# Three feed-forward blocks of a fused kernel: output parts of 6, 8 and 8 chunks, VectorE's order by need, and two of four weight sums made by accumulating transfers

## The chip, the cores and the metric

The kernel runs on one core of one Trainium2 chip. The time is the device time of one execution in microseconds (us), the median of the runs shown. Engines are named as in the profile: PE (TensorE; PEld is its weight load), DVE (VectorE), ACT (ScalarE), POOL (GpSimd) and SP (SyncE, which here only issues transfers).

## The reference, cut to what matters

Two transformer blocks follow each other on a sequence of 512 tokens of width 1024, all in float32. The first has a gated linear attention mixer and a feed-forward block (ffn0); the second a feed-forward block (ffn1), a mixer of pooling and retention, and a feed-forward block (ffn2), then a last norm.

```python
def swiglu_2(x, w1, w3, w2):                       # w1, w3: 1024 x 2816, w2: 2816 x 1024
    return (jax.nn.silu(x @ w1) * (x @ w3)) @ w2

# first block, after its mixer
h = modulate(rms_norm(lat, norm_g[i, 2]), mod_l[:, 3], mod_l[:, 4])
lat = lat + mod_l[:, 5] * rms_norm(swiglu(h, ffn_w_in[i], ffn_w_out[i]), norm_g[i, 3])
# second block
h = h + 0.5 * swiglu_2(rmsnorm(h, ffn1_norm[l]), ffn1_w1[l], ffn1_w3[l], ffn1_w2[l])
...  # mixer
h = h + 0.5 * swiglu_2(rmsnorm(h, ffn2_norm[l]), ffn2_w1[l], ffn2_w3[l], ffn2_w2[l])
return rmsnorm(h, final_norm)
```

## The kernel before, in words

**Numbers in two parts.** Each float32 operand is split into an upper part (ACT copies it to the type fp32r) and a lower part (DVE subtracts the upper from the whole). A product is three matmuls: upper by upper, upper by lower, lower by upper (`mm3`). So every weight tile passes ACT once and DVE once before PE takes it; `hi_done`/`lo_done` count this for whole units, `form_hi`/`form_lo` for forms.

**One ffn** has 11 groups of 256 hidden columns. Groups 0 and 1 (`PLAIN`) are plain: `unit(0, ...)` makes the gate half and `unit(1, ...)` the up half, in ffn0 and ffn1 group 0 runs as `first_pair`, which takes the chunks k of x as they come (`PAIR_ORDER`). Groups 2 to 10 are `pair`s: gate and up weights, each cut into two halves of the inputs (h) and two of the outputs (c), are multiplied with x by Winograd's form of Strassen's scheme, with 7 products of half size instead of 8. Product j takes the weight form j and the x form j (`x_form`). Weight forms 0, 1 and 5 are blocks of the loaded weights as they are. Four are sums, made in place by DVE in `form_sum`: form 3 = block (0,1) + block (1,1), kept in `sum_form[0]`; form 4 = block (0,0) + block (0,1); form 2 = form 4 + block (1,1); form 6 = form 2 + block (1,0), in `sum_form[1]`. `raw_pair[h]` holds the loaded half h of both weights (1 MB each). The 7 x forms need four sums of x quarters (`sum_x`), an upper part by ACT (`x_hi`) and a lower part by DVE (`x_lo`).

**Stretches and output parts.** The pairs run in stretches of 3, 4 and 2; after each stretch an output part multiplies 8, 8 and 6 of the 22 hidden chunks (128 rows of w_out each) with w_out, in four steps jj of 256 output columns, `OUT_PAIRS`. In the third part the last two chunks (group 10) come late: PE does jj 0 and 1 without them, waits for `gated`, and does them after.

**Buffers that tie the engines.** A ring of four slots holds the weight forms. ACT may write form j of a pair when PE has finished the product four forms before (`form_used`). SP loads `raw_pair[0]` of the next pair when DVE has lowered form 4 of this one (`form_lo`), and `raw_pair[1]` when it has lowered form 5. PE takes product 2 of a pair when DVE has lowered form 2 (`form_lo`).

**Order around the change.** Each engine's instructions are written out by hand and run in that order; a wait holds up all that stands behind it on its engine. The changed places are the opening of each ffn on DVE and ACT (from `scale_x` to the first `pair`), `pair` and `first_forms` on DVE, the third output part on PE, the end of ffn0 on DVE, and how the inverse roots of the norm are spread over the partitions before ffn1, the mixer and ffn2 (`broadcast` of a diagonal made by DVE, or `spread_roots` straight from the roots that POOL made). `keep_busy(b, n)` issues n idle matmuls.

## Time and profile before

| | |
|---|---|
| median of 3 runs | 1604.76 us (1600.16, 1604.76, 1604.80) |
| the profiled execution's own time | 1599.87 us |
| its span, first to last instruction | 1598.1 us |
| PE, DVE, ACT, POOL busy | 98%, 70%, 42%, 8% |
| granted TensorE clock, mean | 0.991 |
| moved by DMA | 172 MB, 108 GB/s |

A row of a timeline begins with its start and its duration in us; the bracket at its end is idle time of that engine before the row and what ended it. A row of the waits has the total, the number of waits and the longest. Most of the time lies in matmuls that follow each other without a gap; what can be won without taking matmuls away is in the gaps of PE and in the stretches at half clock.

### The profile page before, as it was taken

How to read it: one execution, taken by the hardware profiler on the slowest of the kernel's cores; microseconds unless marked ns; L12 is line 12 of the kernel's file. 1: busy time of each engine (PE TensorE's matmuls, PEld its weight loads, DVE VectorE, ACT ScalarE, POOL GpSimd, SP SyncE). 2: the span in 40 equal slices, each digit the busy share in tenths (PEclk: the TensorE clock that was granted, in tenths of full speed). 3: DMA queues.
4: the chain of work that ended last, by engine and by line, in shares of the span. 5: the costliest groups of instructions: out<-in, count | busy, mean ns of one | idle time of the engine just before them, and what ended most of it. 6: DMA issues, size and time to landing. Idle time of an engine off the chain costs nothing.

```text
span 1598.1 us, 23120 instructions
## 1 busy us (share of the span) xinstructions
PE 1566.3 (98%) x9784; PEld 1411.7 (88%) x9784; DVE 1113.7 (70%) x1284; ACT 670.6 (42%) x848; POOL 122.4 (8%) x106
## 2 busy tenths in 40 slices
PE   9999999999999999989999999999999999999997
PEld 7888888889989989778989989888988799899896
DVE  5898764688748746788847856666457786587466
ACT  4554375554525514525524533421323354254242
POOL 0100000020000000000000000175006000000000
PEclk9999999999999999999999999999999999999999
DMA  9544511221412322303231332343212222223131
GB/s 387 198 157 158 211 53 53 80 79 54 158 53 106 131 81 93 119 27 99 84 135 55 105 132 80 106 146 105 80 53 80 79 106 106 82 92 145 53 117 69
DMA packets 35879, 172.05 MB, mean 108 GB/s; under 512 B 3008, under 2 KB 5312, under 8 KB 26176
## 3 DMA queue, kind: packets, MB, share of 16 engines
q1 hardware_dynamic: 31424, 153.80, 26.9%
q0 software_dynamic: 4352, 16.78, 3.1%
q8 instruction: 77, 1.26, 0.3%
q14 instruction: 26, 0.21, 0.0%
HBM read 168.47 MB, written 2.10 MB: 107 GB/s over the span
## 4 chain that ended last, share of the span: by engine, by line
PE 86%; DVE 8%; DMA 2%; issue 2%; ACT 1%; POOL 0%; DVEq 0%; POOLq 0%; ACTq 0%
PE bank L585 86%; DMA raw_pair<-in_ffn_in 2%; DVE form_slot L2504 2%; DVE sum_form L2498 1%; DVE hs L2462 1%; DVE raw_pair L2498 1%; ACT form_slot L1709 0%; DVE x_form L2478 0%; DVE unit_slot L2539 0%; DVE both L2451 0%; DVE w_all L1898 0%; DVE kd L2297 0%; DVE both L2277 0%; DVE both L2429 0%; PE bank L940 0%
## 5 line engine op out<-in xcount | busy, mean ns | idle before, releaser
L585 PE MATMUL bank<-x_form,form_slot 128*128 128x256 f32 x4536 | 548.6, 284 | 6.8 <-DVE form_slot L2504 5.4
L585 PEld LDWEIGHTS bank<-x_form,form_slot 128*128 128x128 f32 x4536 | 547.4, 193 | 8.6 <-issue 5.8
L585 PE MATMUL bank<-g_slot,unit_slot 128*128 128x512 f32 (+1 forms) x1614 | 362.2, 385 | 4.8 <-DVE unit_slot L2539 3.0
L585 PEld LDWEIGHTS bank<-g_slot,unit_slot 128*128 128x128 f32 x1614 | 298.3, 188 | 66.0 <-DVE unit_slot L2539 3.9
L1709 ACT ACTIVATE form_slot<-raw_pair 128x1024 fp32r<-128x1024 f32 x135 | 140.8, 1054 | 244.8 <-PE bank L585 147.5
L585 PE MATMUL bank<-a_hi,w_all 128*128 128x512 f32 x768 | 235.9, 396 | 6.6 <-DVE w_all L1898 6.4
L2504 DVE TENSOR_TENSOR form_slot<-raw_pair,form_slot 128x1024 fp32r<-128x1024 f32 x135 | 164.1, 1221 | 64.4 <-ACT form_slot L1709 64.3
L585 PEld LDWEIGHTS bank<-a_hi,w_all 128*128 128x128 f32 x768 | 144.3, 189 | 39.2 <-issue 9.3
L585 PE MATMUL bank<-a_lo,w_all 128*128 128x512 f32 x384 | 142.6, 392 | 0.0
L1898 DVE TENSOR_TENSOR w_all<-w_raw,w_all 128x2048 fp32r<-128x2048 f32 x38 | 90.1, 2371 | 47.4 <-ACT w_all L1378 47.3
L2539 DVE TENSOR_TENSOR unit_slot<-w_raw,unit_slot 128x2048 fp32r<-128x2048 f32 (+1 forms) x36 | 77.0, 2139 | 60.3 <-ACT unit_slot L1728 44.7
L1728 ACT ACTIVATE unit_slot<-w_raw 128x2048 fp32r<-128x2048 f32 (+1 forms) x36 | 63.7, 1770 | 127.6 <-PE bank L585 127.6
L1378 ACT ACTIVATE w_all<-w_raw 128x2048 fp32r<-128x2048 f32 x40 | 76.5, 1912 | 93.5 <-PE bank L585 93.5
L585 PE MATMUL bank<-w_all,a_hi 128*128 128x512 f32 (+1 forms) x384 | 108.8, 359 | 0.0
L490 POOL TENSOR_TENSOR root<-col,power 128x4 f32<-128x4 f32 (+2 forms) x15 | 18.3, 1222 | 977.2 <-DVE col L1925 776.7
L585 PEld LDWEIGHTS bank<-a_lo,w_all 128*128 128x128 f32 x384 | 72.7, 189 | 15.5 <-issue 0.5
L585 PE MATMUL bank<-w_all,a_lo 128*128 128x256 f32 (+1 forms) x256 | 78.7, 308 | 0.0
L585 PEld LDWEIGHTS bank<-w_all,a_hi 128*128 128x128 f32 x384 | 67.7, 189 | 10.2
L2498 DVE TENSOR_TENSOR sum_form<-raw_pair,raw_pair 128x1024 f32<-128x1024 f32 x54 | 66.0, 1222 | 9.9 <-DMA raw_pair<-in_ffn_in 8.7
L2588 DVE SCALAR_TENSOR_TENSOR xT<-bank,xT 128x512 f32<-128x512 f32 x32 | 22.1, 689 | 72.7 <-PE bank L585 72.7
L2504 DVE TENSOR_TENSOR form_slot<-sum_form,form_slot 128x1024 fp32r<-128x1024 f32 x54 | 65.7, 1216 | 9.9 <-ACT form_slot L1709 9.8
L1709 ACT ACTIVATE form_slot<-sum_form 128x1024 fp32r<-128x1024 f32 x54 | 56.5, 1047 | 0.0
(314 smaller groups left out, 1850.1 us busy)
## 6 DMA issues: line engine op xcount, KB each, us to landing
raw_pair<-in_ffn_in SPq DMA_DIRECT2D x54, 1024.0 KB, 5.2
w_raw<-in_ffn_out SPq DMA_DIRECT2D x24, 1024.0 KB, 4.9
mod_raw<-in_mod POOLq DMA_DIRECT2D x16, 1024.0 KB, 5.6
w_raw<-in_ffn_in SPq DMA_DIRECT2D x12, 1024.0 KB, 4.9
w_raw<-in_gla_in SPq DMA_DIRECT2D x10, 1024.0 KB, 5.7
w_raw<-in_mix_in SPq DMA_DIRECT2D x10, 1024.0 KB, 4.9
w_raw<-in_ffn_out SPq DMA_DIRECT2D x12, 768.0 KB, 4.2
mod_w<-in_mod SPq DMA_DIRECT2D x8, 1024.0 KB, 18.2
```

The source lines that it names most:

```text
L490: nc.gpsimd.tensor_tensor(root4[:, c0:c0 + n], col4[:, c0:c0 + n], power[:, 0:n], ALU.pow).then_inc(root_done, 1)
L585: return pe.matmul(out, lhs, rhs, start=first, stop=last, skip_group_check=True)
L1378: nc.scalar.activation(flat(w_hi[s]), flat(w_raw[s]), ACT.Copy).then_inc(hi_done[s], 1)
L1709: nc.scalar.activation(ring[(STRETCH_SLOT[q] + at) % 4][:, 0], form_source(j), ACT.Copy).then_inc(form_hi, 1)
L1728: nc.scalar.activation(flat(unit_slot[(PART_SLOT[q] + 2 * jj) % 4])[:, 0:w], flat(w_raw[s])[:, 0:w], ACT.Copy).then_inc(hi_done[s], 1)
L1898: V.tensor_tensor(flat(w_lo[s]), flat(w_raw[s]), flat(w_hi[s]).bitcast(F32), ALU.subtract).then_inc(lo_done[s], 1)
L2462: V.scalar_tensor_tensor(hs[:, m], xT[:, m], gains(m), roots[:], ALU.mult, ALU.mult).then_inc(hs_done, 1)
L2498: V.tensor_tensor(out, x, y, ALU.add).then_inc(form_summed, 1)
L2504: V.tensor_tensor(slot[:, 1], form_source(j), slot[:, 0].bitcast(F32), ALU.subtract).then_inc(form_lo, 1)
L2539: V.tensor_tensor(flat(unit_slot[(at + 1) % 4])[:, 0:w], flat(w_raw[s])[:, 0:w], flat(unit_slot[at % 4])[:, 0:w].bitcast(F32), ALU.subtrac ...
L2588: done = V.scalar_tensor_tensor(xT[:, m], b[:], 0.5, xT[:, m], ALU.mult, ALU.add)
```

## The change

- Stretches of 2, 4 and 3 pairs, output parts of 6, 8 and 8 chunks; the slots of the ring, of the output weights and of the gated values are moved to fit. In the third part only jj 0 is cut in two around the wait for group 10; jj 1 to 3 run whole.
- Forms 3 and 4 are no longer summed by DVE. SP loads block (0,1) once more, alone, into `sum_form[0]` (two transfers of 256 KB, in pieces of 512 bytes), as soon as form 3 of the pair before is lowered. POOL waits for it and adds block (1,1) from HBM with two accumulating transfers; then it waits for `raw_pair[0]` and adds block (0,0) from HBM onto block (0,1) in it, with two more. ACT's form 3 waits for `sum_moved[0]`, its form 4 and DVE's sum for form 2 for `sum_moved[1]`.
- On DVE the opening of each ffn is put in another order; the x forms 2 to 6 are lowered one by one inside the first pair.
- The roots come by `spread_roots`: in ffn1 after chunk (0,3) instead of (0,5), before ffn2 and the mixer after the fourth product of the second unit instead of the eighth, without the diagonal. The 20 idle matmuls before ffn1 become 8.
- At the end of ffn0 the last output chunk (m = 7) is added after the terms of chunk 6.

VectorE, opening of ffn1: `hs` is `scale_x`, `x_sum` is `sum_x`, `w_all` the lower part of a unit's weights (w_raw_49 for `lo_done[0]`, w_raw_50 for `lo_done[1]`), `x_form` is `x_lo`, `both<-bank,roots` scales a gate or an up half. Before:

```order
L2462 SCALAR_TENSOR_TENSOR hs<-xT,cols,roots 128x512 x8
L2467 TENSOR_TENSOR x_sum<-hs 128x4x256
L2469 SCALAR_TENSOR_TENSOR x_sum<-x_sum,hs 128x4x256
L2471 TENSOR_TENSOR x_sum<-hs,x_sum 128x4x256
L2472 TENSOR_TENSOR x_sum<-hs 128x4x256
L2429 TENSOR_TENSOR both<-bank,roots 128x512 x2
L1898 TENSOR_TENSOR w_all<-w_raw_49,w_all 128x2048
L2440 TENSOR_TENSOR both<-bank,roots 128x512 x2
L2451 TENSOR_TENSOR both<-both 128x1024
L1898 TENSOR_TENSOR w_all<-w_raw_50,w_all 128x2048
```

and now:

```order
L2485 SCALAR_TENSOR_TENSOR hs<-xT,cols,roots 128x512 x8
L2452 TENSOR_TENSOR both<-bank,roots 128x512 x2
L1922 TENSOR_TENSOR w_all<-w_raw_49,w_all 128x2048
L2463 TENSOR_TENSOR both<-bank,roots 128x512 x2
L2490 TENSOR_TENSOR x_sum<-hs 128x4x256
L2492 SCALAR_TENSOR_TENSOR x_sum<-x_sum,hs 128x4x256
L2494 TENSOR_TENSOR x_sum<-hs,x_sum 128x4x256
L2495 TENSOR_TENSOR x_sum<-hs 128x4x256
L2474 TENSOR_TENSOR both<-both 128x1024
L1922 TENSOR_TENSOR w_all<-w_raw_50,w_all 128x2048
```

The weights of the unit that PE takes next now stand ahead of the four sums.

VectorE, from form 6 of one pair to form 4 of the next: `raw_pair_60`, `raw_pair_61` are halves 0 and 1, `sum_form_70` is form 3, `sum_form_71` form 6. Before:

```order
L2504 TENSOR_TENSOR form_slot_63<-sum_form_71,form_slot_63 128x1024
L2504 TENSOR_TENSOR form_slot_64<-raw_pair_60,form_slot_64 128x1024
L2498 TENSOR_TENSOR sum_form_70<-raw_pair_60,raw_pair_61 128x1024
L2498 TENSOR_TENSOR raw_pair_60<-raw_pair_60 128x8x128
L2504 TENSOR_TENSOR form_slot_65<-raw_pair_61,form_slot_65 128x1024
L2523 SCALAR_TENSOR_TENSOR both<-kd_159,ke_160 128x2x256
L2526 TENSOR_TENSOR both<-bank,kd_159 128x2x256
L2498 TENSOR_TENSOR raw_pair_60<-raw_pair_60,raw_pair_61 128x8x128
L2498 TENSOR_TENSOR sum_form_71<-raw_pair_60,raw_pair_61 128x1024
L2504 TENSOR_TENSOR form_slot_62<-raw_pair_60,form_slot_62 128x1024
L2529 TENSOR_TENSOR both<-bank,snap_b 128x2x256
```

and now:

```order
L2520 TENSOR_TENSOR form_slot_62<-sum_form_71,form_slot_62 128x1024
L2520 TENSOR_TENSOR form_slot_63<-raw_pair_60,form_slot_63 128x1024
L2520 TENSOR_TENSOR form_slot_64<-raw_pair_61,form_slot_64 128x1024
L2537 SCALAR_TENSOR_TENSOR both<-kd_160,ke_161 128x2x256
L2540 TENSOR_TENSOR both<-bank,kd_160 128x2x256
L2514 TENSOR_TENSOR raw_pair_60<-raw_pair_60,raw_pair_61 128x8x128
L2514 TENSOR_TENSOR sum_form_71<-raw_pair_60,raw_pair_61 128x1024
```

Two of the four sums are gone from VectorE; the sum for form 2 stays where it was. GpSimd has in their place, once for each of the 27 pairs:

```order
L525 DMA sum_form_70<-in_ffn_in 128x4x128 x2
L528 DMA raw_pair_60<-in_ffn_in 128x4x128 x2
```

The diff, cut:

```diff
-STRETCHES = ((2, 3, 4), (5, 6, 7, 8), (9, 10))
+STRETCHES = ((2, 3), (4, 5, 6, 7), (8, 9, 10))
-OUT_PARTS = ((0, 8), (8, 16), (16, 22))
-PART_SLOT = (1, 1, 0)
-PART_NEEDS = (4, 8, 11)
+OUT_PARTS = ((0, 6), (6, 14), (14, 22))
+PART_SLOT = (2, 2, 0)
+PART_NEEDS = (3, 7, 11)
...
@@ sync, ffn
                         n = PAIRS_PER_FFN * f + i - PLAIN
+                        if n:
+                            sp.wait_ge(form_lo, FORMS * n - 3)
+                        for u in range(2):
+                            sp.dma_start(form_source(3)[:, u], weight_block(w_in, i, 0, 1)[:, u]).then_inc(sum_begun, 16)
                         for h in range(2):
@@ gpsimd
+            def form_sums(f, w_in):
+                for q, groups in enumerate(STRETCHES):
+                    for i in groups:
+                        n = PAIRS_PER_FFN * f + i - PLAIN
+                        pool.wait_ge(sum_begun, begun_before + 32 * (n + 1))
+                        for u in range(2):
+                            pool.dma_start(form_source(3)[:, u], weight_block(w_in, i, 1, 1)[:, u], accum_op=ALU.add).then_inc(sum_moved[0], 16)
+                        pool.wait_ge(raw_loaded[0], 16 * (RAW_BEFORE[f] + i + 1 + 2 * q))
+                        for u in range(2):
+                            pool.dma_start(form_source(4)[:, u], weight_block(w_in, i, 0, 0)[:, u], accum_op=ALU.add).then_inc(sum_moved[1], 16)
@@ tensor, unit
-                    if roots_to is not None and order.index((k, c)) == KD - 1:
-                        broadcast(roots_to, T, tmp[3], roots_spread)
+                    if roots_to is not None and order.index((k, c)) == KD // 2 - 1:
+                        spread_roots(roots_to, 0, roots_spread)
@@ tensor, group
-                        first_pair(*((3 * KD, (0, 5)) if scaled else (2 * KD,)))
+                        first_pair(*((3 * KD, (0, 3)) if scaled else (2 * KD,)))
@@ tensor, third output part
-                    for jj in range(2):
-                        pe.wait_ge(lo_done[jj], cnt.next(lo_done[jj]))
-                        out_banks_free(q, jj)
-                        out_products(q, jj, k0, late)
-                    pe.wait_ge(gated, GROUPS * f + PART_NEEDS[q])
-                    for jj in range(2):
-                        out_products(q, jj, late, k1)
-                        cnt.expect(pair_out[jj])
-                    for jj in (2, 3):
+                    for jj in range(OUT_PAIRS):
                         s = jj % 2
                         pe.wait_ge(lo_done[s], cnt.next(lo_done[s]))
                         out_banks_free(q, jj)
-                        if f == 2 and jj == 3:
-                            out_products(q, jj, k0, k0 + 1)
-                            last_part(s, k0 + 1)
+                        if jj == 0:
+                            out_products(q, jj, k0, late)
+                            pe.wait_ge(gated, GROUPS * f + PART_NEEDS[q])
+                            out_products(q, jj, late, k1)
+                        elif f == 2 and jj == 3:
+                            out_products(q, jj, k0, KF - 5)
+                            last_part(s, KF - 5)
...
-            keep_busy(0, 20)
+            keep_busy(0, 8)
@@ scalar, form_upper
+                    elif j in (3, 4):
+                        act.wait_ge(sum_moved[j - 3], moved_before + 32 * (n + 1))
@@ vector, form_sum (the sums for forms 3 and 4 are gone)
+                        dve.wait_ge(sum_moved[1], moved_before + 32 * (n + 1))
                         dve.wait_ge(form_lo, FORMS * n + 1)
                         out, x, y = form_source(2), form_source(4), form_source(5)
```

## Rows read from the trace of the kernel before

**Rows 1.** The page, part 1: busy time, share and instructions.

```profile
PE 1566.3 (98%) x9784; PEld 1411.7 (88%) x9784; DVE 1113.7 (70%) x1284; ACT 670.6 (42%) x848; POOL 122.4 (8%) x106
```

**Rows 2.** Waits of PE over the span: total us, times, longest.

```profile
PE bank L585 <- DVE w_all L1898: 6.4, 1, 6.4
PE bank L585 <- DVE form_slot L2504: 5.4, 1, 5.4
PE bank L585 <- DVE unit_slot L2539: 3.0, 2, 1.9
PE bank L585 <- DVE qd L2297: 3.0, 1, 3.0
PE bank L585 <- ACT both L1614: 1.8, 1, 1.8
```

**Rows 3.** Timeline of PE from the end of ffn0 into ffn1.

```profile
672.65 2.21 PE L585 MATMUL bank<-g_slot,unit_slot 128*128 128x512 f32 x9
...
680.57 1.05 PE L585 MATMUL bank<-ones,qd 128*128 128x1 f32 x8 [3.03 <-DVE qd L2297]
...
687.09 5.48 PE L585 MATMUL bank<-ones 128*128 128x128 f32 x40
...
706.07 1.05 PE L585 MATMUL bank<-ident,root 128*128 128x128 f32 x8
...
721.70 0.77 PE L585 MATMUL bank<-a_hi,w_all 128*128 128x512 f32 x1 [6.39 <-DVE w_all L1898]
```

**Rows 4.** Timeline of DVE in the same stretch.

```profile
687.40 0.69 DVE L2336 TENSOR_TENSOR y_ffn<-y_ffn,bank 128x512 f32<-128x512 f32 x1 [2.50 <-PE bank L585]
...
702.85 1.63 DVE L2387 SCALAR_TENSOR_TENSOR a_lo<-xT,cols,a_hi 128x512 fp32r<-128x512 f32 x2
707.86 5.39 DVE L2462 SCALAR_TENSOR_TENSOR hs<-xT,cols,roots 128x512 f32<-128x512 f32 x8 [3.38 <-ACT roots L1640]
713.28 1.23 DVE L2467 TENSOR_TENSOR x_sum<-hs 128x1024 f32<-128x1024 f32 x1
...
719.27 2.28 DVE L1898 TENSOR_TENSOR w_all<-w_raw,w_all 128x2048 fp32r<-128x2048 f32 x1
```

**Rows 5.** Stretches: length, busy PE, PEld, DVE, ACT, POOL; granted clock, DMA share, GB/s.

```profile
870.42:890.58 20.16, 20.16 (x171) 20.16 (x169) 16.12 (x15) 11.48 (x13) 0.00 (x0) 1.00 0.31 105
721.70:726.40 4.70, 4.70 (x11) 3.77 (x12) 4.60 (x5) 4.30 (x5) 0.00 (x0) 0.50 0.70 212
1282.08:1286.20 4.12, 4.12 (x19) 4.12 (x20) 4.09 (x5) 1.96 (x2) 0.00 (x0) 0.50 0.00 0
```

**Rows 6.** Timeline of PE in the third output parts of ffn0, ffn1 and ffn2.

```profile
658.26 2.08 PE L585 MATMUL bank<-g_slot,unit_slot 128*128 128x512 f32 x8 [1.79 <-ACT both L1614]
...
1034.28 2.11 PE L585 MATMUL bank<-g_slot,unit_slot 128*128 128x512 f32 x8 [1.10 <-DVE unit_slot L2539]
...
1570.93 1.42 PE L585 MATMUL bank<-g_slot,unit_slot 128*128 128x512 f32 x5 [1.95 <-DVE unit_slot L2539]
```

**Rows 7.** Timeline of DVE at the opening of ffn2.

```profile
1271.52 4.56 DVE L2478 TENSOR_TENSOR x_form<-x_sum,x_form 128x1024 fp32r<-128x1024 f32 x4
```

**Rows 8.** Timelines of DVE and PE in the stretch of four pairs of ffn1.

```profile
876.40 1.23 DVE L2504 TENSOR_TENSOR form_slot<-raw_pair,form_slot 128x1024 fp32r<-128x1024 f32 x1 [0.94 <-ACT form_slot L1709]
...
891.94 1.21 DVE L2498 TENSOR_TENSOR raw_pair<-raw_pair,raw_pair 128x1024 f32<-128x1024 f32 x1
...
917.58 6.01 PE L585 MATMUL bank<-x_form,form_slot 128*128 128x256 f32 x48 [0.72 <-ACT snap_a L1716]
```

**Rows 9.** Tile raw_pair, 856 to 924 us: from SP's issue to landing.

```profile
DMA to landing us min/median/max: 5.5/6.1/7.2
```

**Rows 10.** Tile mod_raw (POOL's own loads, 1 MB each), and POOL's queue on the page.

```profile
L519 POOL DMA_DIRECT2D mod_raw<-in_mod x16: 748/748/952, 49.3 to 175.5; - x16
DMA to landing us min/median/max: 5.4/5.6/7.4
q0 software_dynamic: 4352, 16.78, 3.1%
```

90 lines of the change are left out of this document (51 added, 39 removed).

## The prediction

> **What bounds the kernel now.** I read the page first: PE is busy 98% of a span of 1598.1 us, DVE 70% [rows 1]. The change takes away no matmul of the products, so a gain can only come from PE's idle time, from its half clock and from idle matmuls. Then I read PE's waits: five causes make 19.6 us [rows 2], and the timelines say where each lies. Two are at the openings of ffn1 and ffn2 (6.4 and 5.4 us, for DVE), one at the end of ffn0 (3.0 us, for the last sum over y), three in the third output parts (1.79, 1.10 and 1.95 us) [rows 6]. After the two openings the granted clock is 0.50 for 4.70 and 4.12 us of work [rows 5], after PE had stood still for 6.39 and 5.44 us. Inside a stretch of pairs a pair takes 20.16 us, PE is busy all of it and DVE 16.12 us of it [rows 5].
>
> The profiled execution took 1599.87 us, 1.8 more than its span; the median of the runs is 4.9 higher. I make the sum on the span and set it against the median. A difference of about 0.3% (5 us) is what a measurement of this kernel can tell from no change.
>
> **Third output parts.** Before, PE does jj 0 and 1 without the last two chunks, then both late pieces at once, so that both finish almost together and the weights and banks of jj 2 and 3 are asked for before ACT and DVE have them. Now only jj 0 is cut. One chunk of one jj is 6 matmuls; 9 of this kind take 2.21 us [rows 3], so a chunk takes 1.36 us and a jj of 8 chunks 10.9 us, where one of 6 took 8.2. Behind the last pair, DVE and ACT need for group 10 a combine, silu, product, its upper and its lower part: 0.7 + 1.1 + 1.2 + 1.1 + 1.2, and 0.8 because ACT copies the weights of jj 1 in between: 6.1 us, an estimate, under the 8.2 us of six chunks. The lower weights of jj 1 follow at 8.4, needed at 10.9. Each later jj gives DVE 10.9 us for work that it did in 8.2. All three waits go: 4.8 us; at worst, if group 10 is late by more than 2 us, half of it comes back.
>
> **End of ffn0.** PE's last product ends at 672.65 + 2.21 = 674.86; DVE starts to scale y by the roots at 687.40 [rows 3, 4]: 12.5 us. In between DVE adds chunks 6 and 7, then eight term operations, and only then has PE what it sums. Now chunk 6 and its terms are done while PE still multiplies chunk 7. DVE's queue behind the third jj (2 sums, the lower part of a unit at 2.3 us [rows 4], 8 terms at 0.6) is 8.4 us long, chunk 6 takes another 3.8, so chunk 7 is reached about 1.4 us after PE's end. Its own chain (sum, square on ACT, four DVE operations of 0.6 to 0.7, the root on POOL at 1 to 2 us, a spread of 0.8 to 1.0 us on PE [rows 3]) takes 6.6 to 7.6. That is 8.0 to 9.0 instead of 12.5: a gain of 4, range 2 to 5.
>
> **Opening of ffn1.** I count from the row at 687.40 [rows 4]. Before, 20 idle matmuls (40 pieces in 5.48 us [rows 3]) hold PE until 692.3, the roots are spread at 706.07, DVE scales x from 707.86, then come sums (4 x 1.2 us from 713.28), gates and at 719.27 the weights: PE starts the next unit at 721.70 [rows 3, 4]. Now 8 idle matmuls end at 689.2, under the first upper part of x, so PE starts there. `first_pair` goes at the pace at which DVE delivers x, about 2 us a chunk, up to chunk (0,3), then at PE's own 1.36 us. By that count (0,3) ends at 699.5, the roots are spread by 700.4, and the last step ends at 712.6. DVE is done lowering x at 702.85 + 1.63 = 704.5 and goes on at once: 5.4 for `hs`, 1.2 for the gates, 2.3 for the weights: 713.4. So PE's next unit starts at 713.5 instead of 721.70: 8.2 us, and the wait shrinks to 0.9. The sums now stand behind it: 713.4 + 1.2 (ups) + 4.9 + 1.2 (product) + 2.3 (weights) = 723.0, where PE asks for them at 713.5 + 10.9 = 724.4. Cover of 1.4 us; if it is missed, the gain is 1 to 3 us smaller. Range 5 to 8.5.
>
> **Opening of ffn2.** Before, DVE lowers all x forms (four of them at 1271.52 in 4.56 us [rows 7]) and makes the first forms after them; PE waits 5.4 us [rows 2]. Now five x forms (6 us) and two sums (2.4 us) have left the path ahead of product 0, and the roots come some 3 us earlier, without the diagonal and four products sooner. Form 0 is lowered about 7 us before PE asks for it. Inside the pair DVE then has 5 x forms more to lower, 6.0 us, in 20.16 us of which it uses 16.1 with the four sums [rows 5]; without two of them it is 13.7 + 6.0 = 19.7. Each form comes just ahead of its product, by my count 1 to 3 us. All 5.4 go; range 3 to 5.4.
>
> **Clock.** If PE no longer stands still for 5 to 6 us there, the work of 4.70 + 4.12 us at half clock [rows 5] takes half of that: 4.4 us; range 0 to 4.4.
>
> **Stretches of pairs, two sums by transfer.** The sums leave DVE, 2.4 us of 16.1, but DVE is not what PE waits for, apart from 0.7 us at 917.58 [rows 8] and a like wait after it, of which I count the 0.7. What counts is when the sum for form 2 can start. Take a pair that starts on PE at 870.42: form 4 is lowered at 877.6 and the sum for form 2 of the next pair starts at 891.94 [rows 8], 21.5 us after the pair's start, and PE just bears it. Now at 877.6 SP issues half 0, which lands after 5.5 to 7.2 us [rows 9]; I take 6.3, since the small load of block (0,1) is ahead of it: 883.9, 13.5 us after the start. Then POOL issues two accumulating transfers of 256 KB. No row shows one. The nearest are POOL's own loads of 1 MB: issue 0.75 us, landing 5.6 in the median, 7.4 at most, and 3.1% of the span for 16 of them, or 3.1 us a piece [rows 10]. So 2.5 us are fixed and 512 KB would take 1.6. Bounds: 4.1 us (a plain load of that size), and 0.75 + 2.5 + 3.1 + 3.1 = 9.4 (each byte handled twice, and half 1, which is in flight then, ahead of it). I take 7, nearer to the second since the pieces are 512 bytes. That puts the sum at 20.5 us, 1 before the 21.5 of now. Since form 4 is lowered behind it in DVE's queue, a landing later than that moves the whole loop: each us beyond 21.5 costs about 1 us in each of the 18 pairs that follow another in a stretch. At 4.1 nothing is lost, at 9.4 it is 1.4 x 18 = 25 us. Form 3's transfer has from about 8 us after one pair's start to 20.2, 12 us, and needs the same 4 to 9. Nothing else stands in POOL's queue during an ffn that anyone waits for.
>
> The Trainium skill (Collectives: The Full Stack, "The bandwidth ceiling: the fold count and why AG ≠ RS ≠ AR") says that an add in a DMA engine is slower because each chunk needs two source reads on one ring. By that the 512 KB would take 3.1 instead of 1.6 us, which still fits; no run here shows it yet.
>
> **Sum.** 4.8 + 4 + 8.2 + 5.4 + 4.4 + 0.7 = 27.5 us, less 0.5 for a small new wait: 27. From the span that gives 1571, from the median 1604.8 - 27 = 1578. Since one of three runs and the profiled one lie 4.7 us lower, I say **1577**.
>
> **Rivals.**
> *One opening still waits.* The weights of the second unit of ffn1, or an x form in a first pair, come late. DVE is nearly full there, which speaks for it; the counted cover of 1 to 3 us speaks against. It leaves 8 to 12 us of the two openings with their clock: 1588.
> *The accumulating transfers are slow.* They land 11 us after half 0 instead of 7. Then the sum for form 2 starts at 24.5 us, 3 us late in 18 pairs: 54 us, 1578 + 54 = 1632, slower. It decides at 8 + 27/18 = 9.5 us: above that the kernel is slower than before. For it: 512-byte pieces, a read before each write, two more loads competing. Against: a DMA share of 0.31 now [rows 5].
> *VectorE holds up GpSimd's transfers.* As a mechanism here: POOL writes its descriptors while DVE works nearly without a pause; if each of the two transfers lost 2.5 us, they would land at 12 us and the time be about 1650. Against it: the 16 loads of POOL landed in 5.4 to 7.4 us while DVE was busy with their predecessors [rows 10]. The Trainium skill (SBUF — State Buffer, "SBUF: two separate sides") warns of this for operations of VectorE in its two-port modes.
> *Nothing comes of it:* gains and a landing at the upper bound of 9.4 cancel, 1604.8 - 27 + 25 = 1603.
>
> **How the numbers follow.** Forecast 0.66 (1571 to 1584), one opening waits 0.16 (1584 to 1600), nothing 0.04, transfers slow 0.11, VectorE holds them up 0.03. The low end of the range is the fastest run less the full sum with every term at its best: 1600.2 - 30 = 1570. To leave no more than 2 in 10 out it must reach over the first rival: 1600. Faster 0.82, within 0.3% 0.04, slower 0.14.
>
> **What would show it.** PE's waits have no `w_all`, `form_slot` or `unit_slot` of over 1.5 us; the third parts run through; no half clock after the openings; PE starts the unit behind `first_pair` about 34 us after the end of ffn0's products instead of 46.8. Four accumulating issues per pair on POOL; from half 0's landing to theirs 7 us, and DVE's wait for them before the sum for form 2 is short. Wrong would be: pairs of more than 20.16 us in the stretches with DVE or ACT waiting for a DMA into raw_pair; a wait for form 3; a busy DVE behind PE in the first pairs.

## The result, and the profile after

The changed kernel takes **1631.93 us** in the median of 4 runs (1630.86 to 1636.98), the kernel before 1602.76 beside it: a ratio of 1.0189, 95% interval 1.016 to 1.0218. It is slower by 29 us, where 27 us less were forecast. The profiled execution has a span of 1630.0 us against 1598.1.

The page of the changed kernel: busy time (to be read beside [rows 1]), the software queue, that is GpSimd's (packets, MB, share of the 16 DMA engines' time), and transfers (count, KB each, median us from issue to landing; beside [rows 9] and [rows 10]).

```profile
PE 1579.2 (97%) x9772; PEld 1421.8 (87%) x9772; DVE 1049.7 (64%) x1228; ACT 669.0 (41%) x848; POOL 258.4 (16%) x214
...
q0 software_dynamic: 61376, 45.10, 17.1%
...
raw_pair<-in_ffn_in SPq DMA_DIRECT2D x54, 1024.0 KB, 6.9
...
sum_form<-in_ffn_in SPq DMA_DIRECT2D x54, 256.0 KB, 3.5
sum_form<-in_ffn_in POOLq DMA_DIRECT2D x54, 256.0 KB, 8.8
raw_pair<-in_ffn_in POOLq DMA_DIRECT2D x54, 256.0 KB, 7.7
```

PE's waits in the changed kernel (beside [rows 2]; total us, times, longest):

```profile
PE bank L608 <- ACT snap_a L1737: 34.3, 14, 4.0
PE bank L608 <- ACT snap_b L1737: 3.1, 7, 0.5
...
PE bank L608 <- DVE qd L2321: 1.5, 1, 1.5
...
PE bank L608 <- DVE form_slot L2520: 0.4, 1, 0.4
...
PE bank L608 <- DVE w_all L1922: 0.2, 1, 0.2
```

Read these two ways. The five waits of [rows 2] are gone or halved: `w_all` fell from 6.4 to 0.2, `form_slot` from 5.4 to 0.4, `qd` from 3.0 to 1.5, and the output weights no longer appear. What the change was to win at the openings, it mostly won. But one new wait of 34.3 us in 14 places stands above them. It bears the name of `snap_a`, a copy of a bank that ACT makes ahead of product 2, and rightly so: in all 13 gaps of PE of over 1.3 us in the pairs that copy ends 0.05 us ahead of PE's start. But it stands in ACT's order behind the upper parts of forms 2 and 3, and the one of form 2 waits for VectorE's sum. What that sum waits for, VectorE's own waits show:

```profile
DVE raw_pair L2514 <- issue: 43.8, 17, 5.3
```

L2514 is `form_sum`, and its output `raw_pair` is form 2. In 17 pairs VectorE stood up to 5.3 us ahead of that sum. "issue" says that the profile gives no releaser; what the instruction waits for there are the accumulating transfers (`sum_moved[1]`): in each of the 18 pairs that follow another in a stretch, form 4's second transfer lands 0.08 us ahead of the sum, and in 17 of them VectorE stands idle up to that moment. This is the loop of the changed kernel in the stretch of four pairs of ffn1, SP, POOL, ACT, DVE and PE in turn (start, duration, idle time before and its releaser):

```profile
881.91 0.92 SPq L450 DMA_DIRECT2D sum_form<-in_ffn_in  x2
884.08 2.64 SPq L458 DMA_DIRECT2D raw_pair<-in_ffn_in  x2
...
885.94 2.59 POOL L525 DMA_DIRECT2D sum_form<-in_ffn_in  x2 [16.51 <-DMA sum_form<-in_ffn_in]
891.51 2.59 POOL L528 DMA_DIRECT2D raw_pair<-in_ffn_in  x2 [2.98 <-DMA raw_pair<-in_ffn_in]
...
891.25 1.06 ACT L1730 ACTIVATE form_slot<-raw_pair 128x1024 fp32r<-128x1024 f32 x1 [3.05 <-DMA raw_pair<-in_ffn_in]
896.51 1.06 ACT L1730 ACTIVATE form_slot<-raw_pair 128x1024 fp32r<-128x1024 f32 x1 [3.71 <-DMA raw_pair<-in_ffn_in]
...
904.80 0.58 ACT L1737 ACTIVATE snap_a<-bank 128x512 f32<-128x512 f32 x1
...
901.64 1.23 DVE L2514 TENSOR_TENSOR raw_pair<-raw_pair,raw_pair 128x1024 f32<-128x1024 f32 x1 [1.61 <-issue]
...
905.43 6.78 PE L608 MATMUL bank<-x_form,form_slot 128*128 128x256 f32 x42 [3.36 <-ACT snap_a L1737]
```

SP issues half 0 at 884.08. ACT's form 0 and POOL's second pair of issues start on its landing, POOL's at 891.51, 7.4 us later. Form 3's transfer was issued at 885.94, in between. Half 1 lands at 896.5. Form 4's transfer is issued at 891.51, and VectorE's sum for form 2 starts on it at 901.64, 10.1 us later; PE then waits 3.36 us ahead of product 2: behind the sum ACT makes the upper parts of forms 2 and 3 (902.89 to 904.90) and `snap_a` (to 905.38), and PE starts at 905.43. VectorE's lower part of form 2 was done 0.13 us before that copy. From one issue of half 0 to the next it is 24.45 us (859.63 to 884.08), where a pair took 20.16 [rows 5].

Two stretches of the windows (length; busy PE, PEld, DVE, ACT, POOL; granted clock, DMA share, GB/s) show where the transfers are, and a third what stands behind a wait:

```profile
884.08:896.51 12.43, 11.96 (x100) 11.76 (x100) 6.51 (x6) 4.53 (x7) 5.18 (x4) 1.00 1.04 243
896.51:901.64 5.13, 4.75 (x40) 4.57 (x39) 2.43 (x4) 1.05 (x1) 0.00 (x0) 1.00 0.70 87
...
905.43:909.30 3.87, 3.87 (x20) 3.87 (x21) 2.93 (x4) 2.95 (x3) 0.00 (x0) 0.56 0.00 0
```

From half 0's issue to half 1's landing the 16 DMA engines are full (share 1.04). In the last 5.13 us, with only the accumulating transfers left, they are still busy at 0.70 but move 87 GB/s. And behind the wait of 3.36 us PE worked 3.87 us at a mean granted clock of 0.56, most of it at 1.2 instead of 2.4 GHz. There are nine such stretches of 3.4 us in the pairs of this execution; none is at an opening any more. PE's busy time rose by 12.9 us (1579.2 against 1566.3) although it has 12 matmuls fewer.

### The profile page after: what moved, and what is told of

It reads as the page before. It is cut to its first block, busy times and chain, and to the rows that moved or that the text cites. A ratio compares the mean times of both kernels' runs of the same rounds, so it can differ in the third digit from the quotient of the medians.

```text
span 1630.0 us, 23175 instructions
## 1 busy us (share of the span) xinstructions
PE 1579.2 (97%) x9772; PEld 1421.8 (87%) x9772; DVE 1049.7 (64%) x1228; ACT 669.0 (41%) x848; POOL 258.4 (16%) x214
## 3 DMA queue, kind: packets, MB, share of 16 engines
q0 software_dynamic: 61376, 45.10, 17.1%
## 4 chain that ended last, share of the span: by engine, by line
PE 67%; DMA 13%; DVE 10%; issue 7%; ACT 2%; POOL 1%; DVEq 0%; POOLq 0%; SPq 0%; ACTq 0%
PE bank L608 66%; DMA raw_pair<-in_ffn_in 12%; DVE form_slot L2520 3%; ACT form_slot L1730 2%; DVE raw_pair L2514 1%; POOL raw_pair L528 1%; DVE sum_form L2514 1%; DVE both L2540 1%; DMA sum_form<-in_ffn_in 1%; DVE both L2543 0%; DVE qd L1997 0%; DVE xT L2363 0%; DVE hs L2485 0%; POOL sum_form L525 0%; DVE y_ffn L2360 0%
## 5 line engine op out<-in xcount | busy, mean ns | idle before, releaser
L608 PE MATMUL bank<-x_form,form_slot 128*128 128x256 f32 x4536 | 565.2, 288 | 38.2 <-ACT snap_a L1737 34.3
L608 PEld LDWEIGHTS bank<-x_form,form_slot 128*128 128x128 f32 x4536 | 560.1, 196 | 43.9 <-ACT snap_a L1737 37.1
L525 POOL DMA_DIRECT2D sum_form<-in_ffn_in x54 | 70.2, 1559 | 577.8 <-DMA sum_form<-in_ffn_in 577.8
L1922 DVE TENSOR_TENSOR w_all<-w_raw,w_all 128x2048 fp32r<-128x2048 f32 x38 | 89.8, 2363 | 50.8 <-ACT w_all L1397 50.8
L528 POOL DMA_DIRECT2D raw_pair<-in_ffn_in x54 | 70.1, 1516 | 144.9 <-DMA raw_pair<-in_ffn_in 119.1
L2514 DVE TENSOR_TENSOR raw_pair<-raw_pair,raw_pair 128x1024 f32<-128x1024 f32 x27 | 33.0, 1223 | 46.6 <-issue 43.8
```

Of the source, the lines that this page charges most:

```text
L525: pool.dma_start(form_source(3)[:, u], weight_block(w_in, i, 1, 1)[:, u], accum_op=ALU.add).then_inc(sum_moved[0], 16)
L528: pool.dma_start(form_source(4)[:, u], weight_block(w_in, i, 0, 0)[:, u], accum_op=ALU.add).then_inc(sum_moved[1], 16)
L608: return pe.matmul(out, lhs, rhs, start=first, stop=last, skip_group_check=True)
L1922: V.tensor_tensor(flat(w_lo[s]), flat(w_raw[s]), flat(w_hi[s]).bitcast(F32), ALU.subtract).then_inc(lo_done[s], 1)
L2514: V.tensor_tensor(out, x, y, ALU.add).then_inc(form_summed, 1)
```

## The experiments

All times are medians; the ratio is to the kernel before on the same chip, with its 95% interval. The kernel before took 1602.8 to 1605.1 us on the chips used, so that a difference between rows of two chips is uncertain by about 2 us. The last column is read from the traces: the median, over the 18 pairs that follow another one in a stretch, of the time from SP's issue of half 0 to VectorE's start of the sum for form 2.

| kernel | us | ratio | issue of half 0 to sum, us |
|---|---|---|---|
| kernel before | 1603 | | 13.3 |
| changed kernel | 1631.9 | 1.016 to 1.0218 | 16.3 |
| e1, no transfers | 1580.6 | 0.985 to 0.9884 | 13.8 |
| e1r, the same again | 1581.8 | 0.9833 to 0.9882 | 13.7 |
| e2, before with transfers | 1648.4 | 1.0261 to 1.0295 | 16.3 |
| e3, form 3 alone | 1585.2 | 0.9858 to 0.991 | 14.2 |
| e4, form 4 alone | 1584.8 | 0.9871 to 0.9929 | 13.4 |
| e5, writes without adding | 1601.9 | 0.9966 to 0.9993 | 15.3 |
| e7, form 3 in pieces of 2 KB | 1622.5 | 1.0083 to 1.0132 | 15.9 |
| e8, form 4 first | 1583.9 | 0.985 to 0.9896 | 13.0 |
| e8r, the same again | 1583.3 | 0.9847 to 0.9892 | 13.0 |
| e9, form 3 first, both behind half 0 | 1651.7 | 1.0273 to 1.031 | 17.2 |
| h2, before with form 4 first | 1608.8 | 1.0008 to 1.0033 | 13.3 |
| d1, form 3's transfer halved | 1595.3 | 0.9911 to 0.996 | 14.6 |
| f1, parts undone | 1592.1 | 0.9906 to 0.9934 | |
| f2, end of ffn0 undone | 1582.1 | 0.9833 to 0.9861 | |
| f3, openings undone | 1594.9 | 0.9918 to 0.9964 | |

**Is it the transfers at all?** e1 takes them out of the changed kernel, e2 puts them alone into the kernel before.

```diff
-                        for u in range(2):
-                            sp.dma_start(form_source(3)[:, u], weight_block(w_in, i, 0, 1)[:, u])...
...
-            form_sums(1, a["ffn1_in"])
...
 def first_forms(q, i):
+    form_sum(q, i, 0)
+    form_sum(q, i, 1)
```

> The changed kernel with all four weight sums on VectorE again, in the order of the kernel before; everything else of the change stays (stretches 2, 4, 3, openings, end of ffn0, third output part, roots). Theory (the accumulating transfers alone cost the time, the rest gains what the sum said): 1577 us, 1572 to 1584, and no gap of PE inside a stretch of pairs; the first pair of each ffn may be late by up to 2 us, since VectorE has 16.1 + 6.0 = 22.1 us of work in its 20.16. Rival A (the gains of the openings are not real, the time hangs on something else of the change, such as the new stretches): 1600 us or more. Rival B (both share in it): 1585 to 1600.

> The kernel before with the transfers alone: block (0,1) loaded once more, forms 3 and 4 made by accumulating transfers of GpSimd, VectorE's two sums gone; stretches of 3, 4 and 2 and all openings as before. Theory: the loop from form 4 of one pair to form 4 of the next is about 5 us longer and each stretch loses the same as in the changed kernel, some 55 us with the half clock behind the gaps: 1603 + 55 = 1658, 1645 to 1670. Rival A (the loss comes from the new order and not from the transfers): within 5 us of 1603.

e1 took 1580.6 us, 22.8 less than the kernel before, and e2 1648.4, 45 more. So the transfers cost 45 to 51 us in either surrounding, and the rest of the change brings 23. The order and the stretches are not to blame. e1 came out within its band, e2 as well. e1 has no gap of over 1.3 us in a stretch of pairs; e2 has the wait of the changed kernel again, and the old ones too:

```profile
PE bank L611 <- ACT snap_a L1744: 29.4, 15, 5.3
PE bank L611 <- DVE w_all L1926: 6.4, 1, 6.4
```

**Which of the two?** e3 leaves only form 3 to the transfer, e4 only form 4 (form 3 is then `form_source(3)` plus `form_source(5)` on VectorE).

```diff
-                        pool.wait_ge(raw_loaded[0], ...)
-                        for u in range(2):
-                            pool.dma_start(form_source(4)[:, u], ..., accum_op=ALU.add)...
```

> The changed kernel with form 4 summed by VectorE again and form 3 alone made by the accumulating transfer. Theory (it is form 4's transfer that lies on the loop: half 0 loaded, block (0,0) added, form 2 summed; form 3's has 12 us of its own): 1577 to 1583, no wait in a stretch of over 0.5 us. Rival C (any accumulating transfer slows the loads beside it, so that half 1 comes late): about half of the loss stays, 1600 to 1610, and VectorE waits for half 1 before the sum for form 2.

> The changed kernel with form 3 made by VectorE (block (1,1) added onto the block (0,1) that is loaded alone) and form 4 alone made by the accumulating transfer. Theory (form 4's transfer is the loop): 1620 to 1632, since it still starts only behind half 0 and takes nearly as long. Rival C (the number of accumulated bytes beside the loads counts, not which form it is): about half of the loss, 1600 to 1610.

e3 came out as expected (1585.2). e4 did not: 1584.8 where my theory of that moment said 1620 to 1632 and its rival 1600 to 1610. Each transfer alone costs about 4 us, which is hardly more than the runs of one kernel differ by (e4: 1581.4 to 1592.0), both together 51. The page of e4 shows where it went: form 4's transfer lands 5.1 us after its issue, not 7.7.

```profile
raw_pair<-in_ffn_in SPq DMA_DIRECT2D x54, 1024.0 KB, 6.0
...
raw_pair<-in_ffn_in POOLq DMA_DIRECT2D x54, 256.0 KB, 5.1
```

So form 4's transfer lies on the loop but fits into it. What doesn't fit is form 3's ahead of it. I formed the theory anew: the transfers of a pair, all released within some ten microseconds, fill the DMA engines, and the loop waits for all that stands ahead of form 4's.

**Does the order decide?** e8 swaps the two in GpSimd's queue and changes nothing else; h2 does the same on the kernel before.

```diff
-    (wait for sum_begun, form 3's two transfers)
     (wait for raw_loaded[0], form 4's two transfers)
+    (wait for sum_begun, form 3's two transfers)
```

> The changed kernel with GpSimd's queue in the other order: it waits for half 0 and adds block (0,0) for form 4 first, and only then adds block (1,1) for form 3. Nothing else changes, not the bytes nor the pieces. Theory D with sharing in time (form 3's transfer runs beside half 0 and ahead of form 4's, and that is what delays the loop): form 4's transfer lands within 6 to 7 us of half 0; form 3's lands some 7 us later than before, still ahead of product 3: 1585 to 1600. Rival V (the volume of the added pieces in a pair fills the queues, whatever the order): 1620 to 1635. If form 3 then comes too late, PE waits ahead of product 3, and the time lies between.

> The kernel before with the transfers alone, but with form 4's accumulating transfer ahead of form 3's in GpSimd's queue. In the other order it took 1648.4 against 1603.4. If the order alone decides, here too: 1600 to 1610, the same as the kernel before. If the stretches or the openings of the changed kernel are needed for it: 1615 to 1640.

The swap gives back 48 us: 1583.9, 1 us below my band. On the kernel before it gives back 40, 1608.8 against 1648.4. The same bytes in the same pieces, and nearly the whole loss is gone. In all 27 pairs form 3's transfer lands ahead of form 4's in the changed kernel, and behind it in e8. The timeline of e8, same pair of ffn1, SP, POOL, DVE and PE:

```profile
863.43 2.64 SPq L458 DMA_DIRECT2D raw_pair<-in_ffn_in  x2
...
869.45 2.59 POOL L525 DMA_DIRECT2D raw_pair<-in_ffn_in  x2 [15.91 <-DMA raw_pair<-in_ffn_in]
870.94 3.71 POOL L528 DMA_DIRECT2D sum_form<-in_ffn_in  x2
...
876.91 1.23 DVE L2514 TENSOR_TENSOR raw_pair<-raw_pair,raw_pair 128x1024 f32<-128x1024 f32 x1 [0.23 <-issue]
...
881.37 8.89 PE L608 MATMUL bank<-x_form,form_slot 128*128 128x256 f32 x71 [0.30 <-ACT snap_a L1737]
```

Half 0 takes 6.0 us instead of 7.4 (863.43 to 869.45), and the sum starts 7.5 us behind it instead of 10.1: 4.1 us less in this pair (3.3 in the median), and PE waits 0.30 instead of 3.36. Form 3's transfer is now the late one, and its cover is almost used up. ACT in the same pair:

```profile
879.78 1.06 ACT L1730 ACTIVATE form_slot<-sum_form 128x1024 fp32r<-128x1024 f32 x1 [0.54 <-DMA sum_form<-in_ffn_in]
880.74 0.58 ACT L1737 ACTIVATE snap_a<-bank 128x512 f32<-128x512 f32 x1
```

In all 18 pairs ACT's form 3 starts 0.02 us behind that landing, after a wait of 0.2 to 2.8 us, and `snap_a`, which product 2 needs, stands behind it. So form 3's transfer bears on product 2 already and not only on product 3; PE's waits under `snap_a` are 5.0 us in 5 places here, 1.2 us in e1 and 34.3 us in the changed kernel.

**Does form 3's transfer hurt by sharing with the halves, or by standing ahead of form 4's?** e9 keeps the order of the changed kernel but lets both wait for half 0.

```diff
                         pool.wait_ge(sum_begun, begun_before + 32 * (n + 1))
+                        pool.wait_ge(raw_loaded[0], 16 * (RAW_BEFORE[f] + i + 1 + 2 * q))
```

> The changed kernel with GpSimd's queue in its own order, form 3's transfer ahead of form 4's, but both now wait for half 0; so form 3's transfer can no longer disturb half 0, while it still stands ahead of form 4's. With form 4 first the kernel took 1583.9. Theory F (what costs is that form 3's transfer stands ahead of form 4's in the one queue of GpSimd): half 0 lands in 6 us, 1.4 earlier than in the changed kernel, but form 4's transfer lands 11 to 13 us after it instead of 10.1, and the time stays at 1625 to 1645. Theory S (what costs is that form 3's transfer shares the DMA engines with half 0 and half 1): half 0 comes back to 6 us and a third or more of the loss goes, 1600 to 1612.

1651.7: it is not better but 20 us worse, above theory F's band as well, and theory S falls. Half 0 gained nothing to speak of: from its issue to GpSimd's issue that it releases, the median over the 18 pairs is 6.2 us, 6.1 in the changed kernel. Half 1 did come earlier, 9.1 us behind half 0's issue instead of 10.4, and it helped nothing, since the sum waits for form 4's transfer. That sum starts in the median 10.1 us behind GpSimd's first issue after half 0 instead of 9.7, with form 3's whole transfer now in that time.

```profile
879.73 2.59 POOL L526 DMA_DIRECT2D sum_form<-in_ffn_in  x2 [19.27 <-DMA raw_pair<-in_ffn_in]
881.23 3.75 POOL L529 DMA_DIRECT2D raw_pair<-in_ffn_in  x2
...
893.76 4.52 PE L609 MATMUL bank<-x_form,form_slot 128*128 128x256 f32 x23 [2.63 <-ACT snap_a L1738]
```

I had expected 1.4 us less for half 0. The single pair that I had taken that from was not the typical one.

**Is it the work or the mere presence of form 3's transfer?** d1 keeps its two issues and its place and leaves out half of its addition; e5 keeps all four transfers, leaves out the adding and lets them only write; e7 moves form 3's bytes in longer pieces, and so adds another part of the weights than the reference does.

```diff
 d1: form_source(3)[:, u]      ->  form_source(3)[:, u, 0:2], half of the block
 e5: accum_op=ALU.add          ->  (left out)
 e7: weight_block(...)[:, u]   ->  512 neighbouring columns of the half, contiguous
```

> The changed kernel with form 3's accumulating transfer cut to half of its pieces (half of that addition is left out); as many issues, the same order, form 4's transfer whole. If the work ahead of form 4's transfer counts, 512 added pieces of 65 ns each on 16 engines are 2.1 us less of it per pair, and the sum for form 2 starts 1.5 to 2 us earlier, near the 14.3 us behind half 0's issue that the loop bears: 1590 to 1605. If the mere presence of the transfer counts (its two issues of 1.3 us, its place in the queue): 1625 to 1632.

> The changed kernel in which GpSimd's four transfers of a pair only write and do not add: the two sums are left out (forms 3 and 4 are then block (1,1) and block (0,0)); the same issues, the same bytes from HBM, the same 512-byte pieces. Theory D (an added piece keeps a DMA engine twice as long, so that the two accumulating transfers, half 0 and half 1, all released within 6 us, land late together): pieces as short as those of a plain load, half 0 within 6 us, form 4's transfer within 5 us, and 1578 to 1584. Rival I (GpSimd's issuing, 1.3 us for each of the four, and the small pieces are what is slow): 1600 to 1630. Rival Q (what counts is one more transfer ahead in GpSimd's queue, whatever it does): about 1630.

> The changed kernel in which form 3's load and its accumulating transfer move the same 512 KB each in pieces of 2 KB, from a contiguous part of each half (so form 3 is another sum than the reference's; form 4's transfer is left in 512-byte pieces). If the cost of an added piece is mostly per piece, form 3's transfer is over in a third of the time and the loop gets back most of what form 3's share costs (the kernel with form 4's transfer alone took 1584.8): 1585 to 1595. If it is per byte: 1625 to 1632, as the changed kernel.

d1: 1595.3, as the work ahead of form 4's transfer had it; the sum starts 1.7 us earlier (16.3 to 14.6), where 2.1 us of the engines' time was taken away. Presence alone would have left 1625 to 1632.

e5: 1601.9, far above theory D's 1578 to 1584, in rival I's band though not for its reason, as the issues and the pieces that it blames came out shorter and longer than in the changed kernel (below), and rival Q's 1630 is out. 30 of the 51 us go, and 21 stay with transfers that only write. The page prices it:

```profile
q0 software_dynamic: 12992, 45.10, 8.7%
...
raw_pair<-in_ffn_in POOLq DMA_DIRECT2D x54, 256.0 KB, 5.1
```

The software queue takes 17.1% of 1630.0 us in the changed kernel, 3.1% of 1598.1 in the kernel before [rows 10], 8.7% of 1601.6 here. So 27 pairs of two accumulated forms cost 278.7 - 49.5 = 229 us of all 16 engines, 8.5 a pair or 4.2 for each 512 KB; written plainly they cost 139.3 - 49.5 = 90, or 1.7 each. The comparison has a flaw that the row also shows: the writes are listed as 12992 packets, not 61376, so the pieces aren't the same. GpSimd's issue got shorter too, 0.75 us in e5 where the changed kernel has 1.3 to 1.9. What is the adding's, what the pieces' and what the issue's share can't be parted here.

Where the 21 us that stay come from, the trace of e5 tells, and it isn't form 4's transfer. SP, ACT and DVE in one pair:

```profile
867.69 2.64 SPq L458 DMA_DIRECT2D raw_pair<-in_ffn_in  x2
...
880.22 1.06 ACT L1730 ACTIVATE form_slot<-raw_pair 128x1024 fp32r<-128x1024 f32 x1 [4.08 <-DMA raw_pair<-in_ffn_in]
881.31 1.23 DVE L2520 TENSOR_TENSOR form_slot<-raw_pair,form_slot 128x1024 fp32r<-128x1024 f32 x1 [4.40 <-ACT form_slot L1730]
...
883.66 1.22 DVE L2514 TENSOR_TENSOR raw_pair<-raw_pair,raw_pair 128x1024 f32<-128x1024 f32 x1
```

ACT waits for half 1, VectorE for ACT's form 1, and the sum for form 2 stands behind that in VectorE's order and starts without a wait of its own, in all 18 pairs. Form 4's transfer has landed 2.05 us before it (median). Half 1 lands 11.8 us behind half 0's issue (median of the 18), in e1 8.9 and in the kernel before 7.9. So even plain writes delay the loop by what they take from half 1. This second path lies close behind in the changed kernel too: there half 1 lands after 10.4 us, the work ahead of the sum is done at 14.0 instead of 13.3, and only the rest, to 16.3, is the wait for form 4's transfer.

e7: 1622.5, between the two bands (1585 to 1595, 1625 to 1632) and near the second. Only 9 us come back, and the halves got slower:

```profile
q0 software_dynamic: 40640, 45.10, 15.2%
...
raw_pair<-in_ffn_in SPq DMA_DIRECT2D x54, 1024.0 KB, 7.1
```

The queue's time falls from 278.7 to 15.2% of 1621.2 = 246.4 us, 1.2 a pair, so form 3's 4.2 us have become 3.0: by the byte long added pieces are some 30% cheaper. Over the 18 pairs half 0 now takes 7.3 us in the median instead of 6.1, and half 1 lands 12.4 us behind half 0's issue instead of 10.4. With that it is half 1 that sets the sum here in most pairs: in 12 of the 18 VectorE doesn't wait for form 4's transfer at all. So e7 does not say what form 3's cheaper transfer would bring by itself. Why longer pieces delay the halves I have not tested.

**What do the other parts bring?** f1, f2 and f3 undo one part each in the kernel without transfers (1580.6). They ran on other chips than e1; against the kernel before beside it e1 gained 22.8 us, f1 13.0, f2 22.9 and f3 10.1.

```diff
 f1: -STRETCHES = ((2, 3), (4, 5, 6, 7), (8, 9, 10))   OUT_PARTS = ((0, 6), (6, 14), (14, 22))
     +STRETCHES = ((2, 3, 4), (5, 6, 7, 8), (9, 10))   OUT_PARTS = ((0, 8), (8, 16), (16, 22))
 f2: -if p < 3: y_added(CPU * p + 1)      +y_added(CPU * p + 1)
 f3: -keep_busy(0, 8), spread_roots(...)  +keep_busy(0, 20), broadcast(...); the openings as before
```

> The kernel without transfers (1580.6 us) with the stretches of 3, 4 and 2 pairs and the output parts of 8, 8 and 6 chunks of the kernel before, the third one cut after two steps. The ledger has 4.8 us for this: 1585.4, and PE's three waits for the output weights come back (1.8, 1.1 and 1.9 us). Rival (the new stretches cost or bring something of their own in the pairs): outside 1582 to 1588.

> The kernel without transfers (1580.6 us) in which the last chunk of y in ffn0 is added together with chunk 6 again, ahead of the terms of chunk 6. The ledger has 4 us for this, 2 to 5: 1582.6 to 1585.6, the wait of PE for the last sum of y 3.0 us instead of 1.45, and the half clock behind it longer. Rival (what was won there is only the 1.5 us of the shorter wait): 1582.

> The kernel without transfers (1580.6 us) with the openings as in the kernel before: VectorE's and ScalarE's order there, all x forms lowered ahead of the first pair, the roots by the diagonal and after the eighth product, 20 idle matmuls. The new stretches, the third output part and the end of ffn0 stay. The ledger has 8.2 + 5.4 + 4.4 = 18 us for this: 1598.6. Since only 22.8 of 27 us were gained in all, it could be as little as 14: 1594.6. Rival (the gain came from the stretches and output parts): within 3 us of 1580.6.

f3 is 14.3 us slower (12.7 by the kernels beside them), where the ledger had 18 and its low end 14, and has the waits of the two openings back as they were, 6.4 and 5.5 us. f2 is 1.5 us slower in the median, which is within the spread of the runs (1578.74 to 1583.44 against 1579.93 to 1584.27), and by the kernels beside them it isn't slower at all: the new order at the end of ffn0 brings nothing that shows. f1 is 11.4 us slower (9.8 by the kernels beside them), where the ledger had 4.8 and the band ended at 1588. Its waits say why:

```profile
PE bank L589 <- DVE qd L2301: 4.4, 1, 4.4
PE bank L589 <- DVE unit_slot L2542: 3.0, 2, 1.9
...
PE bank L589 <- ACT both L1618: 1.8, 1, 1.8
```

The three waits for output weights are back with 4.8 us, as the ledger had them. But the wait at the end of ffn0 is 4.4 us instead of 1.5. In f2, with the old order but eight chunks a step, it is 1.1:

```profile
PE bank L589 <- DVE qd L2300: 1.1, 1, 1.1
```

So, as far as one profiled execution of each tells, the gain at the end of ffn0 comes from the output part of eight chunks and not from the new order there, and two terms of my sum were not independent. The profiled spans of f1 and e1 differ by 9.3 us; these waits account for 7.7 of them.

**Do the transfers bring anything in the good order?**

> The kernel without transfers again (1580.6 us), to stand beside the next one on one chip. If VectorE's two sums matter anywhere (the first pairs, where it has 22.1 us of work in 20.16), this one is 1 to 4 us the slower one; if not, it is the same or faster by up to 4 us, since the transfers still slow the loads beside them.

> The changed kernel with form 4's transfer first again (1583.9 us), beside the one without transfers. The theory that VectorE is not the bound expects no gain from its two sums less: 0 to 4 us above the one without transfers.

Side by side on one chip the kernel without transfers took 1581.8 us (0.9833 to 0.9882) and the one with form 4 first 1583.3 (0.9847 to 0.9892). They can't be told apart. The 2.4 us per pair taken off VectorE buy nothing that shows, and 42 MB more are moved for it. The best version is e1: the change without its transfers, 1.3% faster than the kernel before and 3.1% faster than the changed kernel (1580.6 against 1631.9).

## Why the prediction was wrong, point by point

The gains came about nearly as counted: e1, which has them alone, took 1580.6 us against the forecast of 1577. What turned 27 us of gain into 29 us of loss is the term that I had put at nothing lost, the two sums by transfer.

**Third output parts, 4.8 us:** right. None of the three waits of [rows 6] is left, and f1 brings back 4.8.

**End of ffn0, 4 us (2 to 5):** too large, and credited to the wrong part of the change. In the changed kernel PE's last product ends at 693.82 + 1.98 = 695.80 and VectorE starts to scale y at 706.87, 11.1 us later instead of 12.5 [rows 3, 4]; I had 8 to 9.

```profile
693.82 1.98 PE L608 MATMUL bank<-g_slot,unit_slot 128*128 128x512 f32 x8
699.94 1.05 PE L608 MATMUL bank<-ones,qd 128*128 128x1 f32 x8 [1.46 <-DVE qd L2321]
...
697.81 0.68 DVE L2622 TENSOR_TENSOR y_acc<-y_acc,bank 128x512 f32<-128x512 f32 x1
706.87 0.69 DVE L2360 TENSOR_TENSOR y_ffn<-y_ffn,bank 128x512 f32<-128x512 f32 x1 [2.24 <-PE bank L608]
```

VectorE reaches chunk 7 at 697.81, 2.0 us behind PE's end, near the 1.4 that I counted. The chain behind it takes 9.1 us, not 6.6 to 7.6: from PE's sum at 699.94 to the end it is 6.9 as before (680.57 to 687.40 [rows 3, 4]: 6.8), and only the wait ahead of PE's sum was shortened (1.46 us against 3.03). In f3, with the same order there, that chain takes 7.5 us (676.63 to 684.16), inside my 6.6 to 7.6; there the half clock behind PE's wait lasts 3.4 us instead of 6.8, and whether that is the whole difference is not tested.

What this term had wrong is the cause of the gain. From PE's last product of ffn0 to VectorE's scaling of y it is 12.5 us with the old order and old parts, 14.4 with the new order and old parts (f1), 10.1 with the old order and new parts (f2) and 11.1 with both new (e1, the changed kernel), one profiled execution each. The new order shortens it in neither pair; the larger output part does. By my own count a step of eight chunks gives VectorE 10.9 us instead of 8.2, and I used that for the third output parts alone.

**Opening of ffn1, 8.2 us:** right for the stretch that I counted. From that row PE's next unit starts after 25.9 us (732.79), forecast 26, before 34.3, and it waits 0.21 us.

```profile
732.79 0.47 PE L608 MATMUL bank<-a_hi,w_all 128*128 128x512 f32 x1 [0.21 <-DVE w_all L1922]
```

Counted from the end of the products it is 37.0 us, not the 34 that I named as a sign; the 3 are the term above.

**Opening of ffn2, 5.4 us, and clock, 4.4 us:** right as rows. The wait is 0.4 us now. The half clock behind the openings is gone (two windows of the changed kernel, answering the last two of [rows 5]):

```profile
732.79:737.49 4.70, 4.70 (x21) 3.91 (x22) 4.63 (x6) 3.64 (x3) 0.00 (x0) 1.00 0.67 219
1300.60:1304.70 4.10, 4.10 (x36) 4.08 (x35) 2.74 (x3) 3.02 (x4) 0.00 (x0) 1.00 0.00 0
```

Together: e1 gained 22.8 us in the median and 20.0 in the span, of 27. Of the 7 us between sum and span, 2.5 are the end of ffn0 and some 2.6 are waits in the pairs: I counted 0.7 as won and 0.5 as new, and e1, which still has four sums on VectorE, has 3.6 in waits of over 0.4 us (the longest 1.30 ahead of the first pair of ffn1) where before had 1.2. The same two explain why f3 gave back 13.7 us of span and not 18: it ends ffn0 1.5 us sooner than e1 does and has 2.6 us less of waits in the pairs. About 2 us stay unexplained, less than the runs of e1 differ by.

**Two sums by transfer: the step that failed.** I let the sum for form 2 start at t0 + 20.5 us, that is 13.3 us behind half 0's issue: 6.3 for half 0 and 7 for the transfer, where the loop bore 14.3 (the one pair of [rows 8]; the median of before is 13.3). The median is 16.3. Half 0 was right (6.1). The transfer was not: 9.7 in the median instead of 7, just above my upper bound of 9.4 and above the 9.5 from which, by my own text, it decides (medians of the parts, which don't add up exactly). With form 4 first the 7 us were met (median 7.0); they were a choice between two bounds, so that luck had a part in it. So the price of the transfer alone was right, and what was left out is **form 3's transfer ahead of it**. The prediction gave that one "12 us, and needs the same 4 to 9", asked whether it was in time for itself, and not what it did to the other. The upper bound counted half 1 ahead of form 4's transfer and nothing else. I also left out what the transfers do to half 1, which VectorE needs ahead of the same sum: 0.6 of the 3 us by which the sum comes later lie ahead of the wait for form 4's transfer (14.0 against 13.3), and in e5, where half 1 lands at 11.8, all of the delay does.

Counted with the measured prices: in the 17.6 us from half 0's issue to the sum (884.08 to 901.64) lie two halves of 1 MB at 3.1 us [rows 10] and two accumulated forms at 4.2, 14.6 us of all 16 engines. The two windows above have 12.43 x 1.04 + 5.13 x 0.70 = 16.5. With form 4 first, form 3's 4.2 fall away ahead of the sum: 4.1 us were measured in the pair shown. The DMA share of 0.31 [rows 5], which I held against the rival, is a mean over a whole pair; here it is the share of the burst that counts, and that is 1.04.

The cost of a late landing was also too low in kind. "About 1 us in each of the 18 pairs" left out the clock. From d1 to e9 the sum starts 2.6 us later and the kernel takes 56.4 us more: 21.7 us for each us, 1.2 for each pair. PE's busy time, 1579.2 us, shows the clock's part beside e1's:

```profile
PE 1561.1 (99%) x9772; PEld 1407.3 (89%) x9772; DVE 1110.2 (70%) x1282; ACT 669.1 (42%) x848; POOL 118.2 (7%) x106
```

The same 9772 matmuls take 18.1 us longer in the changed kernel, and the span less PE's busy time is 50.8 us against 17.0, 33.8 more: 51.9 us in all, the difference of the spans (1630.0 and 1578.1). The nine stretches of 3.4 us at half clock make some 15 of the 18 (9 x 3.4 / 2, an estimate).

**The rivals.** "The accumulating transfers are slow" named the place, the point of decision and the time (1632), for a landing at 11 us; I gave it 0.11. That its 1632 is the measured time to the microsecond is luck: the landing is 9.7, which by its own rule is 31 us over 1578, or 1609, and the rest comes from half 1 and from the half clock, which it didn't count. What I held for it (two more loads competing) weighed more than what I held against it. "VectorE holds up GpSimd's transfers" isn't borne out: in e8 VectorE does the same work in a shorter pair and the landing is 7.0. GpSimd's issue itself is slower than for its own loads (748 ns [rows 10]):

```profile
L528 POOL DMA_DIRECT2D raw_pair<-in_ffn_in x54: 1273/1301/1877, 355.8 to 1546.3; - x54
```

but d1 and e8 have such issues too (1.2 to 1.9 and 1.3 to 3.0 us), and with the adding left out (e5) the same issues beside the same VectorE took 0.75. The Trainium skill's rule of two source reads (Collectives: The Full Stack, "The bandwidth ceiling: the fold count and why AG ≠ RS ≠ AR") points the right way: I had worked out 3.1 us of the engines for 512 KB by it and 1.6 without; the rows give 4.2 and, for plain writes, 1.7. The trace agrees in direction: 2.5 times instead of two, with other pieces in the two kernels.

## What to carry to other kernels

When work is moved to a queue, price the queue's whole content between the release and the landing that the loop waits for, not each transfer for itself: two transfers that cost about 4 us each alone cost 51 together and 3 or less when the urgent one went first. Look also at the other load that the same instruction needs: with the adding gone, half 1 and not form 4's transfer was the late one. A mean DMA share says nothing of the burst behind one semaphore; read it in the window from that issue to the landing. And put a gap of PE in the sum with the half clock behind it.
